# Requests for the experts' down weights moved from SyncE's queue to ScalarE's

## What is computed

```python
def expert_block(args):
    xb, e = args                                  # 128 rows of one expert
    g = xb @ w_gate[e]                            # 1024 x 512
    u = xb @ w_up[e]                              # 1024 x 512
    return (jax.nn.silu(g) * u) @ w_down[e]       # 512 x 1024
```

## Time and profile before

| | us |
|---|---|
| median of 3 runs | 2420.57 |
| lowest and highest of them | 2417.34, 2421.53 |
| the profiled execution, its own time | 2419.61 |
| its span, first to last instruction | 2417.8 |
| TensorE busy in the span | 2253.7 (93%) |
| VectorE, ScalarE, GpSimd busy | 1219.2, 847.2, 80.7 |
| first queue (SyncE's): bytes, share of the 16 DMA engines' span | 398.68 MB, 46.3% |
| ScalarE's queue | 4.81 MB, 0.6% |

### The profile page before, as it was taken

One profiled execution on the slowest core, in us unless ns is written; L12 is line 12 of the kernel. 1 busy time (PEld: TensorE's weight loads), 2 busy tenths in 40 slices (PEclk: granted clock), 3 DMA queues, 4 the chain that ended last, 5 costly groups with the idle time before them and its releaser, 6 DMA issues.

```text
span 2417.8 us, 31712 instructions
## 1 busy us (share of the span) xinstructions
PE 2253.7 (93%) x11294; PEld 1548.6 (64%) x11294; DVE 1219.2 (50%) x2341; ACT 847.2 (35%) x1553; POOL 80.7 (3%) x84
## 2 busy tenths in 40 slices
PE   7999899999999998999999999999989899887887
PEld 4667567888886766678888877778855333333332
DVE  6574746535525856665435457884443332323234
ACT  4234634323324244633323344473432222212123
POOL 0000000000000000000000000000000111111110
PEclk8999999999999999999999999999999999999999
DMA  7662063233232741043233322213315799999997
GB/s 277 206 204 68 9 208 106 89 95 105 92 92 88 220 128 53 5 119 96 87 105 102 98 87 80 97 62 105 120 61 214 280 394 390 420 388 409 411 399 283
DMA packets 214550, 414.34 MB, mean 171 GB/s; under 512 B 20951, under 2 KB 177377, under 8 KB 197857
## 3 DMA queue, kind: packets, MB, share of 16 engines
q1 hardware_dynamic: 200833, 398.68, 46.3%
q0 software_dynamic: 11520, 8.43, 1.1%
q10 hardware_dynamic: 2016, 4.81, 0.6%
HBM read 420.24 MB, written 25.17 MB: 184 GB/s over the span
## 4 chain that ended last, share of the span: by engine, by line
PE 74%; DMA 9%; DVE 6%; issue 5%; ACT 4%; SPq 1%; DVEq 0%; ACTq 0%; PEldq 0%; PEld 0%; POOL 0%; POOLq 0%
PE bank L770 10%; PE bank L771 10%; PE bank L772 10%; DMA arena<-in_expert_up_w 7%; PE bank L694 7%; PE bank L696 7%; PE bank L695 7%; PE bank L1207 5%; PE bank L1216 3%; PE bank L1208 3%; PE bank L818 2%; PE bank L795 2%; PE bank L644 1%; PE bank L808 1%; DMA arena<-in_w_in 1%
## 5 line engine op out<-in xcount | busy, mean ns | idle before, releaser
L1207 PE MATMUL bank<-arena,xT 128*64 128x512 f32 x560 | 265.6, 631 | 48.2 <-DMA arena<-in_expert_up_w 33.8
L694 PE MATMUL bank<-hT_r,arena_r 128*128 128x512 f32 x704 | 287.0, 408 | 13.0 <-DVE arena_r L1823 6.0
L696 PE MATMUL bank<-hT_r,arena_r 128*128 128x512 f32 x704 | 276.2, 392 | 0.0
L772 PE MATMUL bank<-hT_r,arena_r 128*128 128x512 f32 x704 | 274.0, 389 | 0.0
L1208 PE MATMUL bank<-arena,xT 128*64 128x512 f32 x560 | 265.9, 632 | 0.0
L695 PE MATMUL bank<-arena_r 128*128 128x512 f32 x656 | 257.4, 392 | 0.0
L2515 DVE TENSOR_TENSOR hT<-hT,bank 64x512 f32<-64x512 f32 x80 | 54.8, 685 | 317.0 <-PE bank L1195 217.9
L771 PE MATMUL bank<-arena_r,S_r 128*128 128x512 f32 x528 | 205.4, 389 | 0.0
L1207 PEld LDWEIGHTS bank<-arena,xT 128*64 128x64 f32 x560 | 79.2, 145 | 166.0 <-issue 150.6
L694 PEld LDWEIGHTS bank<-hT_r,arena_r 128*128 128x128 f32 x704 | 133.2, 189 | 68.6 <-issue 19.7
L1216 PE MATMUL bank<-arena,hT 128*64 128x512 f32 x560 | 128.9, 604 | 25.6 <-ACT hT L1765 25.2
(11 more groups left out here) (465 smaller groups left out, 4323.5 us busy)
## 6 DMA issues: line engine op xcount, KB each, us to landing
arena<-in_expert_gate_w SPq DMA_DIRECT2D x32, 2048.0 KB, 15.2
arena<-in_expert_up_w SPq DMA_DIRECT2D x32, 2048.0 KB, 20.6
arena<-in_expert_down_w SPq DMA_DIRECT2D x32, 2048.0 KB, 21.1
arena<-in_w_up SPq DMA_DIRECT2D x88, 512.0 KB, 5.0
arena<-in_w_in SPq DMA_DIRECT2D x68, 512.0 KB, 5.9
arena<-in_w_mod SPq DMA_DIRECT2D x32, 1024.0 KB, 6.9
arena<-in_w_down SPq DMA_DIRECT2D x40, 512.0 KB, 3.9
S<-in_w_mod SPq DMA_DIRECT2D x16, 1024.0 KB, 5.0
```

The source lines that it names most:

```text
L694: mm(b[:, :], w_h, hT_r[:, k, :], start=start, stop=False)
L696: return mm(b[:, :], w_l, hT_r[:, k, :], start=False, stop=stop)
L772: return mm(b[:, :], w_slot(arena_r, i, piece)[:, at:at + P], hi, start=False, stop=stop)
L1207: mm(bank[half][gate0:gate0 + SUB, :], x, expert_weights(slot, 0)[:, k, :], start=k == 0, stop=k == KD - 1)
```

## The change

The requests for the down parts leave SyncE's program, except those of spare blocks, and go to ScalarE's. SyncE asks for the pairs alone, one after the other. ScalarE asks for a down part behind `copy_out` of the block that used this part of the slot last (`load_down`), after a wait for `down1_done` of that block. A DMA that ScalarE asks for goes into ScalarE's own queue. The parts, their sizes and their places in the ring stay as they are; what a slot waits for is the same, with `place_before` as the old `while` loop. SyncE waits once for the products of a pair, not once for each part.

```diff
+        def expert_part(e, slot, m):
+            w = ew[m][bass.ds(e, 1)].rearrange("e (p k) n -> p (e k) n", k=KD if m < 2 else 4)
+            return w, ering[:, 3 * (1 - slot) + m, :].rearrange("p (k n) -> p k n", k=w.shape[1])
+
+        def place_before(q):
+            slot, was = TURN[q] % 2, q - 1
+            while TURN[was] is None or TURN[was] % 2 != slot:
+                if TURN[was] is None and TURN[was - 1] % 2 == slot:
+                    break
+                was -= 1
+            return was
...
                 else:
                     e, slot = g * 8 + TURN[q], TURN[q] % 2
...
-                    for m in parts:
-                        for half in range(2):
-                            sp.wait_ge(s[f"in{half}_done" if m < 2 else f"down{half}_done"], g * TURNS + (was + 1))
+                    was = place_before(q)
+                    for half in range(2):
+                        sp.wait_ge(s[f"in{half}_done"], g * TURNS + (was + 1))
+                    for m in range(2):
                         load_part(e, slot, m, f"w_e{3 * slot + m}")
...
-            load_turn(0, 2, (0, 1))
-            for g in range(BLOCKS // TURNS - 1):
-                for q in range(3, TURNS + 3):
-                    load_turn(g, q, (0, 1))
-                    load_turn(g, q - 1, (2,))
-            for q in range(3, TURNS - 1):
-                load_turn(BLOCKS // TURNS - 1, q, (0, 1))
-                load_turn(BLOCKS // TURNS - 1, q - 1, (2,))
-            load_turn(BLOCKS // TURNS - 1, TURNS - 2, (2,))
-            load_turn(BLOCKS // TURNS - 1, TURNS - 1, (0, 1, 2))
+            load_turn(0, 2)
+            for b in range(3, BLOCKS):
+                load_turn(b // TURNS, b % TURNS)
...
+            def load_down(b):
+                for q in range(TURNS):
+                    if TURN[q] is not None and (b - q) % TURNS == (place_before(q) - q) % TURNS:
+                        n = b + q - place_before(q)
+                        if n < BLOCKS:
+                            e, slot = 8 * (n // TURNS) + TURN[q], TURN[q] % 2
+                            act.wait_ge(s["down1_done"], b + 1)
+                            w, dst = expert_part(e, slot, 2)
+                            act.dma_start(dst, w).then_inc(s[f"w_e{3 * slot + 2}"], 16)
...
             for g in range(1, BLOCKS // 2 - 1):
                 for par in range(2):
                     expert_silu(g * 2 + (1 + par))
                     copy_act(g * 2 + par)
                     copy_out(g * 2 + par, par, g * 16 + 16 * par)
+                    load_down(g * 2 + par)
```

More of the change, by code:

```diff
@@ L401, in build @@
         block = ctx.enter_context(nc.Block())
+        ew = [a["expert_gate_w_2"][0], a["expert_up_w_2"][0], a["expert_down_w_2"][0]]
+        def expert_part(e, slot, m):
[8 more added lines that the diff above has]
+            return was
         @block.sync
@@ L551, in _, with load_turn @@
                     i += 1
-            ew = [a["expert_gate_w_2"][0], a["expert_up_w_2"][0], a["expert_down_w_2"][0]]
             def load_part(e, slot, m, told):
-                w = ew[m][bass.ds(e, 1)].rearrange("e (p k) n -> p (e k) n", k=KD if m < 2 else 4)
-                dst = ering[:, 3 * (1 - slot) + m, :].rearrange("p (k n) -> p k n", k=w.shape[1])
+                w, dst = expert_part(e, slot, m)
                 sp.dma_start(dst, w).then_inc(s[told], 16)
-            def load_turn(g, q, parts):
+            def load_turn(g, q):
                 g, q = g + q // TURNS, q % TURNS
@@ L569, in load_turn @@
                     with sp.If(has_rows > 0):
-                        for m in parts:
+                        for m in range(3):
                             for half in range(2):
@@ L1781, in _ @@
             copy_out(0, 0, None)
+            load_down(0)
             expert_silu(2)
@@ L1784, in _ @@
             copy_out(1, 1, None)
+            load_down(1)
             for g in range(1, BLOCKS // 2 - 1):
```

## The result

| | before | after |
|---|---|---|
| median of the runs, us | 2419.47 (7 runs) | 2428.23 (7 runs) |
| lowest and highest | 2417.34, 2421.53 | 2426.49, 2432.15 |
| the profiled execution, its own time | 2419.61 | 2427.25 |
| its span | 2417.8 | 2425.4 |

The account below looks back on a forecast made before the run. The prediction took the time from asking for a pair to its landing as the bound from 2095 to 2335 us, TensorE mostly before and after. 2419.6 - 0.6 - 3.5 + 15.0 = 2430.5, named as 2431 us, range 2416 to 2446.

Parts of the forecast that it names:

- a down part that was behind a pair now runs through it: Expert stage: two queues take turns in the same engines, so pairs share them with down parts and land later; 15.0 us lost.
- two of the signs that I had named: Expert stage: up parts land later than the 20.6 us median; TensorE's wait for them grows from 33.8 to 45 or more.
- 3 x 5.0 = 15.0 us: Expert stage from 2095 us: 5.0 us, one part's time alone in the engines, paid in each of three refills; 15.0 us slower.
- Total bytes are unchanged, so within a stretch that never runs dry this is paid once: Expert stage: with the engines kept full, the pairs' delay of 5.0 us counts once per stretch, not at every pair.
- The holes, -3.5 and -0.6 us: Where a down request held up a pair: asking 6 us sooner gains 3.5 us in groups 2 and 3, 0.6 in group 0.
- The down request "1.2 us later": Expert stage: ScalarE asks behind its two copies, 1.2 us later than SyncE did; costed at nothing, without cover 5 us in all.
- A: Rival, expert stage: pairs lose nothing to down parts and the holes are gained; faster, 2410 to 2413 us; chance 0.13.
- B: Rival, expert stage: same bytes at the same rate, delay paid once, holes gained; no change, 2417 to 2422; chance with D 0.22.
- C: Rival, expert stage: 5 us paid at nearly each turn, lower clock after longer waits; +25 us and over, 2445; chance 0.12.
- D: Rival, expert stage: engines serve requests in order of asking, so nothing is reordered; 2415 to 2425 us; chance with B 0.22.
- The sum: Whole kernel: 2419.6 - 0.6 - 3.5 + 15.0 = 2430.5 us, named as a median of 2431, 0.4% slower.

Follow-up runs that it names:

- run 4: The kernel before, one queue, with the pair of place 4 in each group asked for ahead of the down part of place 2: 2418.7 us, ratio 0.9996.

## Why the prediction was right, and where it was not

The four pairs of runs that differ only in the change:

| | one queue | two queues | loss |
|---|---|---|---|
| as they are | 2419.5 | 2428.2 | 8.8 |
| three result buffers | 2419.4 | 2426.0 | 6.6 |
| requests of 1 MB | 2425.3 | 2433.0 | 7.7 |
| without GpSimd's transfers | 2389.6 | 2400.5 | 10.8 |

**The mechanism, "a down part that was behind a pair now runs through it": right as far as the runs show.** The loss is there in every pair of runs, also where nothing of GpSimd's is left. The gate-to-up distance grew from 4.5 to 7.3 us in the clean pair, the one without GpSimd's transfers, and there TensorE waits for the up part where it is lost. In the kernels as they are, two of the signs that I had named did not show: the up part lands in 20.3 us in place of 20.6, and TensorE's waits for it are 34.7 us and not 45. Part of the loss comes there through VectorE's waits for scatters, up to 4.4 us at blocks 25 and 35. And no run tells the order of the parts from the 1.5% that the engines lose on the same bytes.

**Its size, "3 x 5.0 = 15.0 us": mis-sized, on two counts.** In the clean pair of runs a pair is later by 2.6 us in the median and not by 5.0, though by 9.4 at block 18. That the down part runs beside a pair for a part of its time only is my reading of this, not shown. And it is not paid once in each of three refills from 2095 on. Of the 7.7 us between the two traces 6.3 were lost by block 18 at 2104 us, the first 3.0 at block 8 by way of TensorE's clock; what came behind it, nearly the whole of the stretch for which I had counted 15.0 - 3.5, added 1.4.

**"Total bytes are unchanged, so within a stretch that never runs dry this is paid once": the condition fails.** The engines do run dry more. From 2170 to 2293 us the rate fell from 415 to 393 GB/s. A pair that lands later frees its slot later, and the next request goes out later, which would explain it; I have not traced each dip to it.

**The holes, -3.5 and -0.6 us: not there as a gain of their own.** The changed kernel fills them, and gives back 2.7 us from block 18 to 24 and less from 29 to 34. But the one-queue run that fills them gained 0.4 us, within the noise: the down part that is overtaken becomes late, 12.9 us in two places. I had asked who waits for the pair and had not asked who waits for what it overtakes.

**The down request "1.2 us later" at no cost: right in sum, wrong in the detail.** ScalarE's request goes out while the first copy is still running. In the changed kernel, ScalarE's timeline, with the wait in brackets:

```profile
2139.54 0.59 ACT L1775 ACTIVATE hT<-bank 64x512 f32<-64x512 f32 x1 [4.11 <-DMA y_scratch<-hT,src_y]
2139.55 0.33 ACTq L1786 DMA_DIRECT2D arena<-in_expert_down_w  x1
...
2156.98 0.59 ACT L1775 ACTIVATE hT<-bank 64x512 f32<-64x512 f32 x1 [3.81 <-PE bank L1218]
2157.03 0.34 ACTq L1786 DMA_DIRECT2D arena<-in_expert_down_w  x1
```

It is not the copy that holds the request up but the wait ahead of the copy: 4.11 us in the first of the two. I had named GpSimd's queue nowhere in the working, though its scatters and gathers take 4.5% of the same engines' time and ScalarE's copy waits for the scatters. That left out a term of perhaps 2.2 us, the gain of three buffers, which is not clear of noise.

**The rivals.** A (the holes decide) is out by run 4. B (throughput only) is out, since the same bytes took 8.8 us longer. The Trainium skill's rule that the forecast weighed (DMA: Bandwidth & Descriptors, "Issuing engines are not separate DMA queues", that asking from several engines saves only the time to ask) is borne out in that there was no bandwidth to win: 423 GB/s from 2104 to 2161 us before, 418 after. But here the second queue had a price. C (nearly each turn of the loop pays, and the clock adds) has the right place for the first step and is too dear. D (nothing reordered) is out by the landing times.

**The sum**, 10.9 us of loss against 8.8, thus came out near partly by luck: 15.0 was too much, 4.1 of gain was not there as such, and the two errors cancel in good part.

## What to carry to other kernels

Before a transfer gets a queue of its own, ask whether the one queue is in the order of use. A hole in the DMA rate is worth only what stands still because of it, and a request moved ahead makes another one late: price both. A chain of waits that names a new releaser after a change is a reason for an experiment, not its result: here it named the scatter for half of the stretch, and with most of those waits away at most a quarter came back.

## What the runs showed that I had not expected

GpSimd's gathers and scatters took 4.5% of the engines' time from 1887 to 2405 us, 23 us, and without them the kernel before is 30.0 us faster (2389.6 against 2419.6 in the runs beside it). The median landing of an up part fell from 20.8 to 16.7 us. For 7.5 MB beside 193 that is a high price, and it lies in the kernel before as well. Why it is 30.0 and not 23 the runs do not show.

Requests of 1 MB with 8 KB for each partition in place of 2 MB with 16 KB cost the kernel before 5.9 us (2425.3 against 2419.4), though each engine moves the same bytes.
